# Five raw weight slots instead of four, seven gate slabs summed earlier, and six modulation slabs taken by TensorE

## What is computed

```python
mod = silu(c) @ ada_w[layer] + ada_b[layer]            # 2048 -> 3 * 2048
shift, scale, gate = split(mod, 3)
h = rms_norm(x, norm_g) * (1 + scale) + shift
proj = h @ w_in                                         # a_q a_k a_v a_g i_q i_k i_w r_q r_f r_i r_g
o_a = dsa_sparse_attention(...) * silu(a_g)             # index scores, top 64 keys, softmax
o_r = rms_norm(hgrn2_recurrence(...)) * silu(r_g)       # chunks of 64 tokens
x = x + gate * (concat([o_a, o_r]) @ w_out)
```

## Time and profile before

| | |
|---|---|
| median of 3 runs | 2611.28 us |
| the profiled execution | 2609.46 us, of which its span is 2607.7 us |
| TensorE busy | 2478.5 us (95%), 11390 matmuls |
| VectorE busy | 1497.1 us (57%) |
| ScalarE busy | 1155.4 us (44%) |
| POOL busy | 97.0 us (4%) |
| mean granted TensorE clock | 0.983 |
| read from HBM | 503.06 MB, 194 GB/s over the span |

### The profile page before, as it was taken

One profiled execution on the slowest core, in us unless ns is written; L12 is line 12 of the kernel. 1 busy time (PEld: TensorE's weight loads), 2 busy tenths in 40 slices (PEclk: granted clock), 3 DMA queues, 4 the chain that ended last, 5 costly groups with the idle time before them and its releaser, 6 DMA issues. The chain is left out here.

```text
span 2607.7 us, 28415 instructions
## 1 busy us (share of the span) xinstructions
PE 2478.5 (95%) x11390; PEld 2046.5 (78%) x11390; DVE 1497.1 (57%) x1781; ACT 1155.4 (44%) x1476; POOL 97.0 (4%) x150
## 2 busy tenths in 40 slices
PE   1999999999789999999999999999999999999998
PEld 1788778877678888888888788887788888888886
DVE  6876868587655545554444644585555454444444
ACT  1545465433444444444343544464444444443332
POOL 1100000010100000000000021100000000000000
PEclk9999999999899999999999999999999999999999
DMA  9975444478245556556555555544555555556554
GB/s 352 345 263 164 153 162 146 162 294 319 97 145 189 187 188 193 187 188 207 194 194 194 170 182 193 173 147 154 169 190 183 192 194 189 187 189 210 193 194 146
DMA packets 186131, 507.04 MB, mean 194 GB/s; under 512 B 17744, under 2 KB 18048, under 8 KB 184720
## 3 DMA queue, kind: packets, MB, share of 16 engines
q1 hardware_dynamic: 174544, 460.07, 52.8%
q0 software_dynamic: 10928, 42.99, 4.6%
q10 hardware_dynamic: 528, 2.16, 0.2%
HBM read 503.06 MB, written 2.10 MB: 194 GB/s over the span
## 5 line engine op out<-in xcount | busy, mean ns | idle before, releaser
L543 PE MATMUL acc<-hi,h 128*128 128x512 f32 x2656 | 1054.1, 397 | 41.8 <-DVE lo L1541 13.4
L545 PE MATMUL acc<-hi,h 128*128 128x512 f32 x2656 | 1042.2, 392 | 0.0
L544 PE MATMUL acc<-lo,h 128*128 128x512 f32 x2656 | 1041.5, 392 | 0.0
L1541 DVE SCALAR_TENSOR_TENSOR lo<-raw,gcols,hi 128x1024 fp32r<-128x1024 f32 (+1 forms) x464 | 568.4, 1268 | 466.4 <-ACT hi L1054 465.4
L1054 ACT ACTIVATE hi<-raw,gcols 128x1024 fp32r<-128x1024 f32 (+1 forms) x464 | 500.7, 1130 | 529.1 <-DMA raw<-in_w_ffn_up 394.7
L1539 DVE TENSOR_TENSOR lo<-raw,hi 128x1024 fp32r<-128x1024 f32 (+1 forms) x388 | 454.6, 1214 | 403.7 <-ACT hi L1054 403.2
L1054 ACT ACTIVATE hi<-raw 128x1024 fp32r<-128x1024 f32 (+1 forms) x388 | 387.5, 1048 | 555.5 <-DMA raw<-in_w_ffn_down 289.7
L543 PEld LDWEIGHTS acc<-hi,h 128*128 128x128 f32 x2656 | 504.4, 190 | 151.8 <-issue 26.4
L545 PEld LDWEIGHTS acc<-hi,h 128*128 128x128 f32 x2656 | 503.1, 189 | 107.0
L544 PEld LDWEIGHTS acc<-lo,h 128*128 128x128 f32 x2656 | 504.2, 190 | 102.2 <-issue 0.2
L543 PE MATMUL acc<-hi,g_hi 128*128 128x512 f32 x704 | 274.5, 390 | 1.1 <-DVE lo L1539 1.1
(11 more groups left out here) (314 smaller groups left out, 1080.0 us busy)
## 6 DMA issues: line engine op xcount, KB each, us to landing
raw<-in_w_ffn_gate SPq DMA_DIRECT2D x176, 512.0 KB, 3.8
raw<-in_w_ffn_up SPq DMA_DIRECT2D x176, 512.0 KB, 4.7
raw<-in_w_ffn_down SPq DMA_DIRECT2D x176, 512.0 KB, 4.7
raw<-in_w_in SPq DMA_DIRECT2D x144, 512.0 KB, 4.5
raw<-in_w_kv SPq DMA_DIRECT2D x64, 512.0 KB, 4.7
raw<-in_ada_w SPq DMA_DIRECT2D x32, 512.0 KB, 6.1
ada_raw<-in_ada_w POOLq DMA_DIRECT2D x32, 512.0 KB, 6.2
gate_raw<-in_ada_w POOLq DMA_DIRECT2D x32, 512.0 KB, 8.0
```

Source lines behind the costliest of these rows:

```text
L543: pe.matmul(o, l_hi, w_hi[:, c], start=first, stop=False)
L544: pe.matmul(o, l_hi, w_lo[:, c], start=False, stop=False)
L545: mm = pe.matmul(o, l_lo, w_hi[:, c], start=False, stop=last)
L1541: ins = vec.scalar_tensor_tensor(out=lo[:, r, c], in0=raw[:, r, c], scalar=gcols[:, st.gain, k:k + 1], in1=hi[:, m % HI_SLOTS, c], op0=ALU ...
```

## The change

Five edits that belong together.

- **Five raw slots.** RING is 5. The fifth slot's 8 KB come from the scratch of POOL's dynamic transfers, which is cut to 8192 bytes; base goes down to 8448 and all tiles move. HI_SLOTS stays at 4.
- **The first sixteen modulation slabs.** Twelve go through the raw ring (N_RING = 12), four (early_raw) into free parts of proj; SyncE issues the first of them before w_in slab 0 and three behind it. VectorE sums ten of them. TensorE takes six, PE_ADA = (2, 5, 8, 11, 13, 15), straight from the raw slab: for each of eight output columns two matmuls of one column with a 128 x 128 block of the slab as weights and a column of c as the moving side, accumulated in acc with the turned sums of the others (ada_direct). Scales lie in banks 0, 1 and 2, and the first product waits bank by bank for them to be read.
- **Shift and scale** are formed in steps (first_scales), 1 is added to the scale's bias ahead of time, and h of a pair of k is made as soon as its scale is ready.
- **The gate slabs.** Seven of the sixteen are summed before slab 73: GATE_AT gives the slab ahead of whose conversion each is summed, GATE_IN the buffer. The first four use one buffer, and each is issued once the one before it is summed; the next three use another one.
- **POOL's small transfers** go out behind modulation slab 18, and VectorE's copy of chunk_causal waits for them.

```diff
-RING = 4
+RING = 5
-    base = 16640
+    base = 8448
-    RAW0, HI0, X0, A0, G0, S0 = 0, 32, 64, 80, 112, 200
+    RAW0, HI0, X0, A0, G0, S0 = 0, 40, 72, 88, 120, 208
+    early_raw = [at(f"early_raw{i}", [P, SLAB], slot(2 + i)) for i in range(4)]
...
-    N_ADA, N_MOD, N_RING = 48, 32, 16
-    T_GATE0 = 73
+    N_ADA, N_MOD, N_START, N_RING = 48, 32, 16, 12
+    PE_ADA = (2, 5, 8, 11, 13, 15)
+    SCALE_BANK = (0, 1, 2, 2)
+    GATE_AT = (52, 54, 56, 58, 66, 68, 72, 73, 75, 77, 79, 81, 83, 85, 86, 87)
+    GATE_IN = (0, 0, 0, 0, 3, 3, 3, 0, 1, 2, 0, 1, 2, 0, 1, 2)
     def ada_until(m):
-        if m < T_GATE0:
-            return min(N_RING + max(0, 16 * (m - 1) // 18), N_MOD)
-        return min(N_MOD + m - T_GATE0 + 1, N_ADA)
+        gates = sum(t <= m for t in GATE_AT)
+        if m == 0:
+            return N_RING + 1
+        return N_MOD + gates if gates else min(N_START + max(0, 16 * (m - 1) // 18), N_MOD)
...
+        def wait_summed(a):
+            if a in PE_ADA:
+                sp.wait_ge(ada_taken, PE_ADA.index(a) + 1)
+            else:
+                sp.wait_ge(ada_added, added(a + 1))
...
-                    if s == 0 or st is st_pool:
+                    if m == 0:
+                        pe.wait_ge(mod_ready, (1, 2, 4, 4)[b])
+                    elif s == 0 or st is st_pool:
...
-        pe.wait_ge(xn_ready, TT)
-        for i in range(4):
-            turn_xn(i).then_inc(turned, 1)
-        ada_columns(0, acc[:, 2, 0:8])
-        ada_columns(1, acc[:, 3, 0:8])
-        pe.wait_ge(mod_ready, 1)
+        def ada_direct(a, cols, f, first=False, last=False):
+            for part in range(2):
+                k, b = 2 * (a % 8) + part, part * GW + f * P
+                ins = pe.matmul(cols, ada_slot(a)[:, b:b + P], c_col[:, k:k + 1], start=first and part == 0, stop=False,
+                                skip_group_check=True)
+            if last:
+                ins = pe.matmul(cols, ada_sum[a // 8][:, f * P:(f + 1) * P], ones[:, 0:1], start=False, stop=True,
+                                skip_group_check=True)
+            return ins
...
+        for a in PE_ADA[:-1]:
+            if a < N_RING:
+                pe.wait_ge(raw_landed[a % RING], 32 * (a // RING + 1))
+            else:
+                pe.wait_ge(early_landed[a - N_RING], 32)
+            if a == 8:
+                pe.wait_ge(ada_added, added(4))
+            for f in range(8):
+                ins = ada_direct(a, shift_col(f) if a < 8 else scale_col(f), f, f in BANK_FIRST[a < 8] and a in (2, 8))
+            ins.then_inc(ada_taken, 1)
+            if a == 8:
+                pe.wait_ge(ada_added, added(8))
+                for f in range(8):
+                    ins = pe.matmul(shift_col(f), ada_sum[0][:, f * P:(f + 1) * P], ones[:, 0:1], start=False, stop=True,
+                                    skip_group_check=True)
+                ins.then_inc(ada_turned, 1)
+                pe.wait_ge(xn_ready, TT)
+                for i in range(4):
+                    turn_xn(i).then_inc(turned, 1)
+        pe.wait_ge(early_landed[N_START - 1 - N_RING], 32)
+        pe.wait_ge(ada_added, added(N_START))
+        for f in range(8):
+            ins = ada_direct(N_START - 1, scale_col(f), f, last=True)
+            if f in (1, 3, 7):
+                ins.then_inc(ada_turned, 1)
...
-        ada_to(8)
+        ada_to(7)
...
-        ada_to(16)
-        modulation(0, acc)
-        for i in range(3):
+        ada_to(10)
...
+        ada_to(13)
+        conv_to(0)
+        ada_to(N_START)
+        first_scales(2, 0, 2)
+        first_scales(3, 2, 4)
+        first_scales(4, 4, 8)
+        split_modulated(0)
+        for i in (1, 2):
...
+            vec.wait_ge(phase_in, 16 * 3)
             step(vec.tensor_copy(mask_i[:], chunk_causal[:]))
...
+            if a == N_START + 2:
+                early_rows()
...
+        gate_slab(N_MOD, head_turned, 2 * TT)
+        for a in range(N_MOD + 1, N_MOD + 4):
+            gate_slab(a, ada_added, added(a))
+        gate_slab(N_MOD + 4, a_scored, 8)
...
+        gate_slab(N_MOD + 5, ada_added, added(N_MOD + 5))
+        gate_slab(N_MOD + 7, r_klturned, 4)
+        gate_slab(N_MOD + 6, ada_added, added(N_MOD + 6))
+        gate_slab(N_MOD + 8, r_summed, 4)
+        gate_slab(N_MOD + 9, r_summed, 4)
+        for a in range(N_MOD + 10, N_ADA):
+            gate_slab(a, ada_added, added(a - 2))
+            if a == N_MOD + 10:
                 pool.wait_ge(r_ss_ready, 1)
...
-    nc = bacc.Bacc("TRN2", target_bir_lowering=False, num_devices=1)
+    nc = bacc.Bacc("TRN2", target_bir_lowering=False, num_devices=1, dynamic_dma_scratch_size=8192)
```

More of the change, by code:

```diff
@@ L305, in ada_slot, with added @@
     def ada_slot(a):
-        return raw[:, a % RING] if a < N_RING else ada_raw[(a - N_RING) % 3] if a < N_MOD else gate_raw[(a - N_MOD) % 3]
+        if a < N_START:
+            return raw[:, a % RING] if a < N_RING else early_raw[a - N_RING]
+        return ada_raw[(a - N_START) % 3] if a < N_MOD else gate_raw[GATE_IN[a - N_MOD]]
+    def added(a):
+        return 2 * (a - sum(p < a for p in PE_ADA))
     use, done_no = {}, {}
@@ L323, in build @@
     raw_landed = [sem(f"raw_landed{r}") for r in range(RING)]
+    early_landed = [sem(f"early_landed{i}") for i in range(4)]
+    ada_taken = sem("ada_taken")
     ada_landed = [sem(f"ada_landed{r}") for r in range(3)]
-    gate_landed = [sem(f"gate_landed{r}") for r in range(3)]
+    gate_landed = [sem(f"gate_landed{r}") for r in range(4)]
     ada_added, ada_turned, mod_ready = sem("ada_added"), sem("ada_turned"), sem("mod_ready")
@@ L472, in _, with early @@
                 sp.dma_start(dst, src).then_inc(raw_landed[a % RING], 16)
+        def early(first, last):
+            for a in range(first, last):
+                for part in range(2):
+                    src, dst = ada_part(a, part)
+                    sp.dma_start(dst, src).then_inc(early_landed[a - N_RING], 16)
+        early(N_RING, N_RING + 1)
         for m in range(N_SLABS):
@@ L476, in _ @@
             r = place(m) % RING
+            if m == 1:
+                early(N_RING + 1, N_START)
             if m < RING:
-                sp.wait_ge(ada_added, 2 * (place(m) - RING + 1))
+                wait_summed(place(m) - RING)
             else:
@@ L1523, in ada_to @@
         def ada_to(a):
[L1525 to L1527 removed]
+            while ada_next[0] < a:
+                if ada_next[0] not in PE_ADA:
+                    ada(ada_next[0])
+                ada_next[0] += 1
         def conv(m):
@@ L1603, in split_modulated, with modulation, first_scales @@
                               h_hi[:, :, k, :], ALU.subtract).then_inc(h_ready, 2)
[L1605 to L1611, removed]
-            vec.scalar_tensor_tensor(out=gs[:, c], in0=gs[:, c], scalar=1.0, in1=gcols[:, N_MIX, c], op0=ALU.add,
-                                     op1=ALU.mult).then_inc(mod_ready, 1)
+        def modulation():
+            c = slice(8, 16)
+            vec.wait_ge(ada_turned, 5)
+            step(vec.tensor_tensor(sh[:, c], wk[:, 2, 0:8], gcols[:, B_SHIFT, c], ALU.add))
+            vec.wait_ge(ada_turned, 6)
+            step(vec.tensor_tensor(gs[:, c], wk[:, 3, 0:8], gcols[:, B_SCALE, c], ALU.add))
+            vec.tensor_tensor(gs[:, c], gs[:, c], gcols[:, N_MIX, c], ALU.mult).then_inc(mod_ready, 1)
+        def first_scales(signal, first, last):
+            vec.wait_ge(ada_turned, signal)
+            for k in range(first, last):
+                ins = vec.tensor_scalar(gs[:, k:k + 1], acc[:, SCALE_BANK[k // 2], k % 4:k % 4 + 1],
+                                        gcols[:, B_SCALE, k:k + 1], gcols[:, N_MIX, k:k + 1], ALU.add, ALU.mult)
+            ins.then_inc(mod_ready, (last - first) // 2)
         def row_scale(j):
@@ L2240, in _ @@
+        for a in range(N_START, N_MOD):
+            if a < N_START + 2:
+                pool.wait_ge(early_landed[3], 32)
+            elif a == N_START + 2:
+                pool.wait_ge(ada_turned, 4)
             else:
-                pool.wait_ge(ada_added, 2 * (a - 2))
+                pool.wait_ge(ada_added, added(a - 2))
             for part in range(2):
                 src, dst = ada_part(a, part)
-                pool.dma_start(dst, src).then_inc(ada_landed[(a - N_RING) % 3], 16)
```

78 lines of the change are left out of this document (41 added, 37 removed).

## The result

The changed kernel takes 2569.44 us (median of four runs, 2568.12 to 2572.82), where the kernel before, run beside it, takes 2610.99: a ratio of 0.9846, with a 95% interval of 0.9834 to 0.9857. I had forecast 2590, 2578 to 2604. The sign is right; the gain is 41.6 us instead of 21. The profiled execution took 2569.91 us, its span is 2567.9, so 39.8 us of span are to be found.

A forecast was written before the change was run, and what follows sets the result against it. TensorE, busy 95% of the span, was taken as the bound, with gains only in its waits, head and clock. Terms 0 - 7 - 5 + 0.7 - 4.7 - 1.4 - 3.7 = -21.1 us gave 2588.4, forecast 2590, range 2578 to 2604.

The forecast's parts named there:

- Head: Start up to TensorE's first product: start at 70 to 71 us, worth 0, from -3 to +4 us.
- First rival: Head: direct matmuls run at full clock, so it ends 9 us before now, 2581 in all; chance 0.10.
- Out stage, first h: Out stage's first h: fewer gate slabs and an earlier raw slab leave 1 us of waiting; -7 us.
- Slab 83: ScalarE's raw-slab wait at 606.52 us: with one gate in two slabs nothing waits; -5 us.
- Gate sum at slab 58: VectorE's sum before conversion 58 fills 1.90 us of idle and pushes the rest; +0.7 us (0 to +2.6).
- (a) to (c): Fifth slot lets conversions start earlier: second products -4.7, small stage's kiT -1.4, k stage at 1482.73 us -3.7.
- my two terms of 3 and 1.7: K stage: 3 us of the shorter waits for lo L1541, and a clock dip of 1.7 behind; taken as -3.7.
- The seams: Waits at seams for bands or x hang on gains, sums and rstd, not on a landing: 0.
- Second rival: Fifth slot buys nothing: (a) to (c) are 0, gate slabs alone remain, 2603; chance 0.20.
- Third rival: Early gate slabs: their single buffer turns the sum into a wait, costing 47 us, 2637; chance 0.06.
- Fourth rival: Halved scratch holds POOL's transfers back; undoing the out stage's relief costs 12 us, 2602, with 0 likelier; chance 0.04.

The follow-up runs named there:

- e2: Changed kernel, but w_in slab 4 and all later slabs issued only once the slab four places before is used up, as with four slots: 2602.78 us, 0.998.
- e3: Changed kernel with the sixteen gate slabs back at slabs 73 to 88, one for each slab, in three buffers: 2574.73 us, 0.9871.
- e5: Changed kernel with four of 422 weight slabs (75, 227, 230, 291) issued one slab later, as with four raw slots: 2589.69 us, 0.9936.
- e1: Kernel before with the fifth raw slot alone (new tile places, scratch of 8192 bytes), nothing else of the change: 2574.25 us, 0.9872.
- e9: Gates back at slabs 73 to 88 in a kernel with four TensorE modulation slabs, reordered head, gate sum at 60: 2569.42 us, against 2561.63 without that edit.
- e7: Changed kernel with four TensorE modulation slabs, fourth gate sum at slab 60, 72 unused matmuls ahead of the wait for bands: 2569.39 us, 0.9854.
- e6: Changed kernel with four TensorE modulation slabs, plus seven and two unused float32 matmuls in two waits ahead of the first product: 2563.68 us, 0.9834.

## Why the prediction was right, and where it failed

**Head, forecast 0, first product at 70 to 71.** Right, at 69.17, and by its steps: slab 2 at 17.7 to be used (forecast 19), 417 GB/s from 10 to 20 us, 6.96 to 6.99 us for a slab of direct matmuls (6.8), slab 8 at 33.1 (34.2), no gap from there. The spell of full clock behind the transposes is what the term hung on. It came in the changed kernel's first profile, in which the slab at 46.80 took 4.07 us and not 7; in the rerun it didn't: there the same slab took 6.83 us, the first rise of the clock on record is at 75.3, and the first product came at 71.97, in e2 at 73.59. (The records of the clock begin with its first rise; up to there the profile's clock column says 1.00, and only the lengths of the matmuls show the half clock.) I had worked out 73.2 without it. The same kernel does both, 3 us apart, so that 69.17 and not 72 is in part luck. The Trainium skill, "TensorE: Matmul & The Clock Gate", section "What's actually happening", says that the number of slow matmuls at a start differs between runs of one kernel; these two profiles agree with that, with a first rise at 47.7 and at 75.3 us.

**First rival, direct matmuls at full clock (0.10).** Refuted: 0.50 while nothing but them ran for 12 us. The row at 63 that I set against it is 3 us long and stands behind a wait of 12.19, so it was weaker evidence than I made of it.

```profile
51.00:63.00 12.00, 12.00 (x59) 12.00 (x59) 3.73 (x7) 1.93 (x4) 2.24 (x4) 0.50 1.03 419
```

**Out stage, first h, -7.** The size was right (-7.5), and that was luck, for only one of its causes works. I gave it to three things at once: seven gates gone, the raw slab one slab earlier, nine gates for sixteen slabs. With the gates back and the slot kept (e3) it stays gone; with the gates early and the slot's lead taken away (e2) it is back at 5.5 us; with slab 75 alone late (e5) 4.9 of the 7.5 are back. It belongs to the fifth slot, the second of the three. In the changed kernel slab 75 still lands late, after 9.1 us, and converts just at its landing:

```profile
533.21 2.01 ACT L1128 ACTIVATE hi<-raw 128x1024 fp32r<-128x1024 f32 x2 [7.03 <-DMA raw<-in_w_out]
536.41 0.60 ACT L1211 ACTIVATE proj<-acc 128x512 f32<-128x512 f32 x1 [1.19 <-PE acc L581]
```

But its end is 1.19 us ahead of TensorE's first bank, instead of behind the last one. The transfer is as slow as it was, and costs nothing here because the lead is larger.

**Slab 83, -5.** Right: -6.3, and the early gates do it (e1, e3, e9).

**Gate sum at slab 58, +0.7.** +1.1: the cause right, the size low. The dip of the clock behind this wait, 1.5 us, was in the kernel before as well.

**The fifth slot, (a) to (c), -9.8.** Measured -13.7: the mechanism is the one I named. The waits for proj L1839 went whole and not by 70%, with the dip behind them; of the one for kiT 0.6 us stayed; in the k stage 4.9 us went at one place, about my two terms of 3 and 1.7, of which I had counted 3.7 without saying why.

**The seams, 0.** This is the step that failed, "those at the seams that are for bands or x hang on chains of gains, sums and rstd, not on a landing: 0", and it is 8.7 us. It holds for bands (8.9 us before and after) and for the longest wait for a low part with a gain (4.9 and 5.0), but not for x: those waits, 6.0 us in two, are gone with the fifth slot alone (e1) and back, at 7.2, with slabs 227 and 291 late (e5). I read "released by x" in TensorE's waits, followed it to gains, sums and rstd, and stopped there, with "not on a landing". The row to read was one link further back: what ScalarE did ahead of the squares of that group. It was a conversion, and 0.02 us before it its slab had landed, as for 355 of the 426 conversions of the kernel before (50 with the fifth slot alone). The wait of 1.1 at the end, behind such a conversion at 2581.45, I had left out, and the dip of the clock at m = 20 too: it is 6.9 us long in the two runs at the pace of four slots and 3.4 in the twelve others, with TensorE never idle there, and why is not shown.

**Second rival, the slot buys nothing (0.20).** Refuted by e1, by 32.6 us.

**Third rival, the single gate buffer (0.06).** No wait: the first of those slabs landed 8.4 us after its issue, with time to spare, and the three that had to wait for the one before, between 364 and 397 us, 5.3 to 5.5, not 8.0. VectorE waited 1.6 us in all for gate_raw, after 520 us.

**Fourth rival, the scratch (0.04).** Nothing seen: e1 with half the scratch has all of the slot's gain, and e2 with it equals the kernel before to 0.2%.

What stays open: in which executions the spell of full clock comes in the head, and whether a dip of 3.4 us follows a wait of 1.5 to 4 us. Both vary between runs of like kernels and are worth 3 and 1.7 us each. Open too is the dip at m = 20.

## What to carry to other kernels

When a ring's slots and a converter's slots are equal in number, most conversions start at their landing (five in six here), and the latency of one transfer (5 us here) stands in the in-order queue ahead of whatever comes next. One slot more costs 8 KB in each partition and here moved it off the path at every seam at once, so count all places where an evacuation stands behind a conversion, not only those where the wait names a landing. To test it, make single slabs late: four of 422 gave back 18 us.

## What the runs showed of the hardware

- Float32 matmuls of one column did not bring TensorE to full clock, dense as they were: 12 us without a gap at 0.50, 0.22 us a record. In a spell at full clock 32 of these records took 4.07 us instead of 6.99.
- Float32 matmuls of 128 and 256 columns in a wait did hold or raise the clock (1.00 over a wait of 8.9 us in e7; up at 57.4 us in e6), but it fell again behind a wait of 1.6 us and 1.4 us of one-column matmuls (e6).
- A float32 matmul of 128 columns against ident took 0.113 us a record and two records, at full clock.
- The scratch of POOL's dynamic transfers at 8192 bytes, with 64 transfers of 512 KB and some small ones through it, cost nothing that these runs can tell.
- Eight small transfers, 0.46 MB, issued together with the first large ones, delayed the landing of the third slab by 5 us (17.6 to 22.6), though the bytes are worth about 1.1 us at 415 GB/s.
